# A fused two-block transformer layer: norm sums of queries and keys in two fp32r passes, and the softmax's last product on GpSimd

## The reference, cut to what matters

```python
q_ca = rmsnorm_2(hs(q_ca, N_CA_HEADS), g_q[l])     # x * rsqrt(mean(x*x over 64) + eps) * g
k_ca = rmsnorm_2(hs(k_ca, N_CA_HEADS), g_k[l])
s = einsum('bnqhd,bnkhd->bnhqk', qc, k_band) * d ** -0.5 + bias
p = softmax(where(valid, s, NEG_INF))
out = einsum('bnhqk,bnkhd->bnqhd', p, v_band)
```

## Time and profile before

| | |
|---|---|
| median of 3 runs | 955.28 us (955.16 to 955.39) |
| the profiled execution | 955.42 us |
| its span | 953.7 us |
| PE busy | 941.1 us (99%) |
| DVE, ACT, POOL busy | 691.2, 565.2, 103.8 us |
| TensorE clock granted | full in all 40 slices |
| chain that ended last | PE 86%, DVE 9%, ACT 3% |

### The profile page before, as it was taken

The page is one execution under the profiler, slowest core; times in us unless marked ns, Lnnn a source line. Parts: engine busy times, 40 slices in busy tenths (PEclk is TensorE's granted clock), DMA queues, the critical chain, the costliest instruction groups (busy, mean ns, idle before and its releaser), DMA issues.

```text
span 953.7 us, 13305 instructions
## 1 busy us (share of the span) xinstructions
PE 941.1 (99%) x4712; PEld 786.3 (82%) x4712; DVE 691.2 (72%) x1278; ACT 565.2 (59%) x1115; POOL 103.8 (11%) x215
## 2 busy tenths in 40 slices
PE   8999999999999999999999999999999999999998
PEld 7878998888888887877788877898888888888887
DVE  6487888878788766667768886856544853673988
ACT  6448787753223257479987664556745634644562
POOL 5001212211121103000000000110000000000110
PEclk9999999999999999999999999999999999999999
DMA  8233222149798743733442423365867567586773
GB/s 302 89 112 108 69 79 89 55 157 354 284 322 278 190 142 127 300 111 100 133 166 73 127 67 131 146 167 133 212 207 180 168 192 189 122 234 193 169 186 111
DMA packets 34963, 156.71 MB, mean 164 GB/s; under 512 B 5273, under 2 KB 5529, under 8 KB 22226
## 3 DMA queue, kind: packets, MB, share of 16 engines
q1 hardware_dynamic: 21106, 103.64, 31.6%
q0 software_dynamic: 11152, 49.29, 20.9%
q10 hardware_dynamic: 2640, 2.93, 0.9%
HBM read 144.61 MB, written 5.27 MB: 157 GB/s over the span
## 4 chain that ended last, share of the span: by engine, by line
PE 86%; DVE 9%; ACT 3%; issue 1%; DMA 1%; ACTq 0%; POOL 0%; DVEq 0%; POOLq 0%
PE psum L2276 26%; PE psum L2278 25%; PE psum L2277 25%; PE psum L2423 2%; PE psum L2450 2%; PE psum L2479 1%; PE psum L2474 1%; DVE wl L1318 1%; DVE p_sb L1518 1%; DMA raw<-in_wall 1%; DVE ptl L1537 1%; PE psum L2712 1%; DVE hl L1357 1%; DVE xt L1353 1%; DVE ah L1464 1%
## 5 line engine op out<-in xcount | busy, mean ns | idle before, releaser
L2276 PE MATMUL psum<-hh,wh 128*128 128x512 f32 (+2 forms) x736 | 277.7, 377 | 0.7 <-DVE hl L1357 0.6
L2278 PE MATMUL psum<-hh,wl 128*128 128x512 f32 (+2 forms) x736 | 270.2, 367 | 0.0
L2277 PE MATMUL psum<-hl,wh 128*128 128x512 f32 (+2 forms) x736 | 270.0, 367 | 0.0
L1318 DVE TENSOR_TENSOR wl<-raw,wh 128x512 fp32r<-128x512 f32 x336 | 218.7, 685 | 37.6 <-ACT wh L733 37.0
L733 ACT ACTIVATE wh<-raw 128x512 fp32r<-128x512 f32 x336 | 193.3, 621 | 68.3 <-PE psum L2278 65.2
L2276 PEld LDWEIGHTS psum<-hh,wh 128*128 128x128 f32 x736 | 138.5, 188 | 24.5 <-DVE hl L1357 1.8
L2278 PEld LDWEIGHTS psum<-hh,wl 128*128 128x128 f32 x736 | 138.4, 188 | 23.0
L2277 PEld LDWEIGHTS psum<-hl,wh 128*128 128x128 f32 x736 | 138.7, 188 | 20.5 <-issue 1.2
L2276 PE MATMUL psum<-wh,ah 128*128 128x512 f32 x192 | 76.1, 396 | 0.4 <-ACT p_sb L879 0.4
L2278 PE MATMUL psum<-wh,al 128*128 128x512 f32 x192 | 74.9, 390 | 0.0
L2277 PE MATMUL psum<-wl,ah 128*128 128x512 f32 x192 | 74.8, 389 | 0.0
(11 more groups left out here) (372 smaller groups left out, 1748.6 us busy)
## 6 DMA issues: line engine op xcount, KB each, us to landing
raw<-in_wall SPq DMA_DIRECT2D x79, 1024.0 KB, 5.4
raw<-in_wall POOLq DMA_DIRECT2D x20, 1024.0 KB, 8.1
wa<-in_wada POOLq DMA_DIRECT2D x24, 512.0 KB, 5.8
gt<-in_wada POOLq DMA_DIRECT2D x20, 512.0 KB, 6.9
xt<-in_xcols SPq DMA_DIRECT2D x8, 264.0 KB, 7.9
cb<-c_rows SPq DMA_DIRECT2D x8, 264.0 KB, 3.2
x<-in_x SPq DMA_DIRECT2D x4, 512.0 KB, 11.9
x_kept<-x SPq DMA_DIRECT2D x4, 512.0 KB, 2.6
```

The source lines that it names most:

```text
L1318: e.tensor_tensor(lower_, raw_of(w, c), upper_.bitcast(F32), ALU.subtract).then_inc(v["wl"], 1)
L2276: e.matmul(out_, lh, rh, start=start, stop=False, skip_group_check=True)
L2277: e.matmul(out_, lh, rl, start=False, stop=False, skip_group_check=True)
L2278: return e.matmul(out_, ll, rh, start=False, stop=stop, skip_group_check=True)
```

## The change: what it does

1. `blk` becomes fp32r. After the square ACT also copies it as fp32r into `sq_hi` (upper part), and 2 steps after the set's end (`LAG_LOW`) DVE subtracts that from the square into `sq_lo`. PE sums with two fp32r matmuls instead of one float32 matmul.
2. The lags grow: sum 2 to 4, root 3 to 5, norm 4 to 6 steps.
3. `normalize` of the CA heads moves from ACT (age 6) to POOL (age 5), as a `tensor_scalar` in float32 in place; the turn on PE waits for `g["norm"]`.
4. POOL's other work of the stage is now written into a loop over the steps: table blocks at steps 17, 33, 49, ..., the first value row at 31, `strip` at 72. A semaphore is shared to make room (`ss`), another renamed (`norm`).

```diff
-        LAG_SUM, LAG_ROOT, LAG_NORM = 2, 3, 4
+        LAG_LOW, LAG_SUM, LAG_ROOT, LAG_NORM = 2, 4, 5, 6
...
                     e.activation(sq[:, sub, :], bank[sub], ACT.Square).then_inc(a["sq"], 1)
+                    e.wait_ge(a["sq"], 4 * p + 2 * sub + 1)
+                    if p or sub:
+                        e.wait_ge(t["ss"], 2 * p + sub)
+                    e.activation(sq_hi, sq[:, sub, :], ACT.Copy).then_inc(a["sq"], 1)
...
+                if n - LAG_LOW in SQUARES:
+                    p, sub = SQUARES[n - LAG_LOW]
+                    e.wait_ge(a["sq"], 4 * p + 2 * sub + 2)
+                    if p or sub:
+                        e.wait_ge(t["ss"], 2 * p + sub)
+                    e.tensor_tensor(sq_lo, sq[:, sub, :], sq_hi.bitcast(F32), ALU.subtract).then_inc(v["ss"], 1)
                 if n - LAG_NORM in SQUARES:
...
+            def normalize(h, i):
+                mx, su, nmx = small(h, i)
+                e.wait_ge(v["rcp"], n_score(h, i))
+                e.tensor_scalar(block_p(h, i), block_p(h, i), mx, None, ALU.mult).then_inc(g["norm"], 1)
+
+            table_mask(8)
+            table_mask(9)
+            for n in range(steps_s):
+                if n == 31:
+                    first_value_row()
+                if n == 72:
+                    whole_sticks()
+                if n > 16 and n % 16 == 1:
+                    for x_ in beats_s[first_s[n - 17]:first_s[n - 1]]:
+                        if x_ and x_[0] == "S" and x_[2] == 0 and x_[1] + 2 in CA:
+                            table_mask(x_[1] + 2)
+                for b_ in range(first_s[n], first_s[n + 1]):
+                    x_ = beats_s[b_ - 5] if b_ > 4 else None
+                    if x_ and x_[0] == "S" and x_[1] in CA:
+                        normalize(*x_[1:])
...
                 if h in SB:
                     e.wait_ge(v["scan_s"], n_sb(h, i0))
+                elif h in CA:
+                    e.wait_ge(g["norm"], 12 + n_score(h, i0) - 32)
...
-                    e.wait_ge(a["sq"], 2 * p + sub + 1)
+                    e.wait_ge(v["ss"], 1 + 2 * p + sub + 1)
...
-                    e.matmul(bank[2], blk[:, :], sq[:, sub, :], start=True, stop=True).then_inc(t["ss"], 1)
+                    e.matmul(bank[2], blk[:, :], sq_hi, start=True, stop=False)
+                    e.matmul(bank[2], blk[:, :], sq_lo, start=False, stop=True).then_inc(t["ss"], 1)
```

More of the change, by code:

```diff
@@ L190, in program @@
         ones = sb("ones", [128, 128])
-        blk = sb("blk", [128, 128])
+        blk = sb("blk", [128, 128], F32R)
         eps = sb("eps", [128, 1])
@@ L205, in program @@
         br.close()
+        bq = ExitStack()
+        sb("under_q", [128, 3072], where=bq)
+        parts_q = sb("sq_parts", [128, 2, SEQ], F32R, where=bq)
+        bq.close()
         gt = sb("gt", [128, 2, D])
@@ L278, in program @@
         sq = two
+        sq_hi, sq_lo = parts_q[:, 0, :], parts_q[:, 1, :]
         v_rows = (rows[:, 3072:3584], rows[:, 3840:4352], v_end[:, 0:512], rows[:, 1024:1536])
@@ L920, in at @@
                     return flat[b_ - age] if b_ >= age else None
-                if (x_ := at(AGE["norm"])) and x_[0] == "S" and x_[1] not in SB:
+                if (x_ := at(AGE["norm"])) and x_[0] == "S" and x_[1] in FG:
                     normalize(*x_[1:])
@@ L1034, in keep @@
             def keep(i):
-                e.wait_ge(g["rs1"], 3 * i + 3)
+                e.wait_ge(g["norm"], 3 * i + 3)
                 e.activation(x1[:, i, :], scaled[:, i % 2, :], ACT.Copy, scale=sm[:, 128 + 2 * i:129 + 2 * i]).then_inc(a["xk"], 1)
@@ L2196, in _ @@
                 e.wait_ge(a["nsq"], 2 * i + 1)
-                e.tensor_scalar(r[:, 0:1], m1, EPS, None, ALU.add).then_inc(g["rs1"], 1)
+                e.tensor_scalar(r[:, 0:1], m1, EPS, None, ALU.add).then_inc(g["norm"], 1)
                 e.wait_ge(a["nsq"], 2 * i + 2)
[L2199 to L2202, removed]
+                e.wait_ge(g["norm"], 3 * i + 1)
+                e.tensor_scalar(r[:, 1:2], r[:, 0:1], EPS, m2, ALU.mult, ALU.add).then_inc(g["norm"], 1)
+                e.wait_ge(g["norm"], 3 * i + 2)
+                e.tensor_tensor(r, r, half[:, 0:2], ALU.pow).then_inc(g["norm"], 1)
             gate(0)
@@ L2206, in _, with table_mask @@
             e.wait_ge(v["m"], 24)
-            for h in CA:
+            def table_mask(h):
                 e.wait_ge(d[f"bt{h % 2}"], 16 * (h // 2 - 3))
                 e.memset(bt[h % 2][0:64, 448:512], NEG).then_inc(g["bt"], 1)
[L2210 to L2222, removed]
+            def first_value_row():
+                for j in range(4):
+                    e.wait_ge(d[f"x{4 + j}"], 32)
+                e.wait_ge(v["tile"], 48)
+                e.memset(dv[0][0:1, :], 0.0).then_inc(g["strip"], 1)
@@ new lines, in whole_sticks @@
+            def whole_sticks():
+                e.wait_ge(v["qn"], 8)
+                e.wait_ge(v["tile"], 40)
+                e.memset(strip[:, 0:384], 0.0).then_inc(g["strip"], 1)
+                e.memset(strip[:, 384:512], 1.0).then_inc(g["strip"], 1)
+                e.wait_ge(g["strip"], 3)
+                e.affine_select(out=strip[:, 384:512], in_=strip[:, 384:512], compare_op=ALU.is_ge, fill=0.0, base=0,
+                                pattern=[[1, 128]], channel_multiplier=-1).then_inc(g["strip"], 1)
```

14 lines of the change are left out of this document (7 added, 7 removed).

## The result

| | before | changed |
|---|---|---|
| median of 7 runs each, same chip | 955.39 us | 958.18 us |
| ratio | | 1.0028 (1.0019 to 1.0038) |
| profiled execution; its span | 955.42; 953.7 | 958.56; 956.8 |

A forecast was written before the change was run, and what follows sets the result against it. TensorE was taken as the bound. Terms −3.27 + 0.1 + 0.4 + 1.2 + 0.2 + 1.96 − 0.2 = +0.4 us on the profiled 955.42 gave 955.8, a median of 955.7 us; range 953.0 to 958.2.

The forecast's parts named there:

- (b): Rival: GpSimd's products and VectorE's splits and scores hinder each other, so norms come late; 958.5 us, chance 0.20.
- The sums: Eight norm sums on PE: two fp32r matmuls take 0.455 us instead of 0.863 for one float32; −3.27 us.
- Steps 16 and 24: PE waits there for the first and second norm, late on VectorE; +0.1 and +0.4 us.
- Head 8's first score: Step 33: PE arrives earlier but the copy of the keys' lower part hardly does; idle 0.82 to 2.0 us, +1.2.
- Head 8's first turn: Turns on PE wait for a POOL product, taken as 0.87 us for 512 columns; +0.2 us (0 to 1.0).
- Step 68: The last sum now stands directly before it, so PE waits 2.37 us instead of 0.41; +1.96 us.
- My own test: Forecast wrong as a whole if PE's waits between 395 and 475 us sum to under 2.5 or over 7 us.
- (a): Rival: waits at the norms and head 8's first score are absorbed, only step 68 costs, 1.2 us; 953.0 us, chance 0.23.
- (c): Rival: GpSimd's product takes 1.17 us or more, so turns wait at each of eight heads; 956.9 us, chance 0.10.
- Relief of ScalarE: ACT loses about 17.8 us of normalize and gets eight copies; a split wait may go; −0.2 us (−0.4 to +0.3).

The follow-up runs named there:

- keys_first: Changed kernel with ScalarE writing the keys' upper part ahead of the root and VectorE their lower part ahead of the norm; 955.13 us, ratio 1.0000.
- pool_only: Changed kernel with the norm sums as before (one float32 matmul, lags 2, 3, 4), products still on GpSimd; 955.50 us, ratio 1.0000.
- sums_only: Changed kernel with the softmax's last product back on ScalarE, two-pass sums and long lags kept; 959.38 us, ratio 1.0042.
- mid_f32_act: Changed kernel with lags 2, 3, 4, 5 for seven sums, the eighth float32 with lags 2, 3, 4, products on ScalarE; 958.19 us, ratio 1.0027.
- last_mid: Changed kernel with the eighth sum alone one step earlier (lags 2, 3, 4, 5); 957.93 us, ratio 1.0026.
- gap_before: Kernel before with longer lags (4, 5, 6) for the eighth norm sum only, still float32; 958.47 us, ratio 1.0028.
- last_short: Changed kernel with lags 1, 2, 3, 4 for the eighth sum only, still two fp32r passes; 956.04 us, ratio 1.0005.
- fill: Changed kernel plus five fp32r matmuls with unread results between the eighth sum and step 68; 956.85 us, ratio 1.0013.

## Why the prediction was right, and where it was wrong

The time lies in the range, 0.02 us from its upper end, and there by luck: that end was set near the value of rival (b), whose mechanism is not there. The forecast itself, 955.7, missed by 2.5 us; a kernel slower by over 0.2%, which came out, had a chance of 0.24.

- *The sums.* Right: L2752 and L2753 start 0.24 and 0.22 us ahead of what follows them, and a sum saves 0.41.

```profile
401.60 0.40 PE L2752 MATMUL psum<-sq_parts,blk 128*128 128x512 f32 x1
401.84 0.39 PE L2753 MATMUL psum<-sq_parts,blk 128*128 128x512 f32 x1
402.06 0.39 PE L2314 MATMUL psum<-hh,wh 128*128 128x512 f32 x1
```

- *Steps 16 and 24.* Right in mechanism: VectorE's norm passes end at 404.86 and 411.19, and the steps start behind them, at 404.92 and 411.25.

```profile
404.12 0.74 DVE L1814 SCALAR_TENSOR_TENSOR qk<-psum,prm,two 128x512 f32<-128x512 f32 x1
...
410.45 0.74 DVE L1814 SCALAR_TENSOR_TENSOR qk<-psum,prm,two 128x512 f32<-128x512 f32 x1
```

- *Head 8's first score.* Right: 1.7 for 2.0; keys_first shows the chain that it names.
- *Head 8's first turn.* The term that was mis-sized by five times. I took 0.87 us for a product of 512 columns between bounds of 0.53 and 1.17; the real ones of 512 columns took 1.73 us on average, above both, by form (count, sum, mean ns):

```profile
L2244 POOL TENSOR_SCALAR p_sb<-p_sb,sm 128x512 f32<-128x512 f32 x8 | 13.8, 1725 | 44.5 <-DVE sm L1518 44.5
L2244 POOL TENSOR_SCALAR p_sb<-p_sb,sm 128x384 f32<-128x384 f32 x8 | 11.4, 1422 | 2.6 <-DVE sm L1518 2.6
L2244 POOL TENSOR_SCALAR p_sb<-p_sb,sm 128x256 f32<-128x256 f32 x8 | 9.0, 1130 | 1.5 <-DVE sm L1518 1.4
L2244 POOL TENSOR_SCALAR p_sb<-p_sb,sm 128x128 f32<-128x128 f32 x8 | 5.9, 735 | 1.3 <-DVE sm L1518 1.2
```

The place was right, and it takes both, the length and the place. The reciprocal (425.58) stands behind the norm (424.92), the product starts at 425.85, and the turn waits until 427.49; in pool_only, where the reciprocal is ahead of the norm, the same product costs nothing:

```profile
424.92 0.75 DVE L1814 SCALAR_TENSOR_TENSOR qk<-psum,prm,two 128x512 f32<-128x512 f32 x1 [1.38 <-ACT two L1117]
425.58 0.15 DVE L1518 RECIPROCAL sm<-sm 128x1 f32<-128x1 f32 x1
...
427.49 0.33 PE L2490 MATMUL psum<-ident,p_sb 128*128 128x128 f32 x1 [0.77 <-POOL p_sb L2244]
```

The Trainium skill's 0.77 us for 512 columns, which it gives as a best case ("GPSIMD Engine Reference", §3.1), is half of what one of these took that stands alone (1.57 us at 445.91). Spans on GpSimd are rough in such traces, but the turn that waits (425.85 to 427.49, 1.64 us) bears this one out.

- *Step 68.* The wait is 2.41 for 2.37. **The step that failed is what follows from it**: I ended the account when PE starts again, at full speed. The clock that PE was granted behind the gap was half for 3.4 us, 1.56 us more. My own test, PE's waits summing to under 7 us, could not have found it, since they sum to about 5.3, and the 1.2 that it gives for the kernel before should be 1.6.
- *The rivals.* (a) fails: step 68 costs 2.0, not 1.2, and the wait before the first score grew from 0.8 to 1.7. (b) gives nearly the measured time by a mechanism that is not there: VectorE's splits between 421 and 510 us take 685 ns on average where they took 679, though GpSimd computes beside them; the subtraction has 737 on average for four, one of 0.87 and three of 0.69 among them. The subtraction at 446.88 starts a microsecond after a product has begun, right after ScalarE's copy that it needs, and takes its usual 0.69:

```profile
445.91 1.57 POOL L2244 TENSOR_SCALAR p_sb<-p_sb,sm 128x512 f32<-128x512 f32 x1 [4.47 <-DVE sm L1518]
...
446.88 0.69 DVE L1804 TENSOR_TENSOR sq_parts<-two,sq_parts 128x512 fp32r<-128x512 f32 x1 [0.27 <-ACT sq_parts L1149]
```

The Trainium skill ("SBUF — State Buffer", Terms) describes a lock held for a whole instruction, in which the loser fully blocks; VectorE as the loser for a product of 1.6 us is not what these rows show. (c) was right that the product is slow, and wrong on the place: only one turn waits, not one at each head.
- *Relief of ScalarE.* Hardly felt in the sum, but sums_only and mid_f32_act show that without it the change costs 1.2 us more (2.8 up to step 68, before the clock) and 2.2 us more: it pays for the copies that the two-pass sum brings.

## What to carry to other kernels

A matmul that is made cheaper by splitting its input lengthens the chain in front of it; price that chain from the last result to the consumer, queue by queue, before choosing a lag: here a lag too short cost 0.7 us a sum, one too long cost the wait behind it. A wait of PE as long as those here (2.1 us and more) should be priced with a clock term: here it was nothing in some executions and 1 to 3 us in others. Where the wait couldn't be removed, matmuls into a free bank within it kept the clock up. And an "issue" wait is worth following to the transfer that ends it: one exchange of order on VectorE and ScalarE won 1.9 us there, over half of what the eight sums save.

## What the runs showed of the hardware

- Kernels whose profile shows a wait of PE of 2.1 to 2.4 us had a lower mean clock (0.998 or less) in part of their executions: 7 of 7 (changed), 8 of 10 (last_mid), 5 of 11 (keys_first), 4 of 7 (gap_before). With 2.6 us in sums_only it was 1 of 5, with two more at 0.999. Where the longest wait is 1.7 us (last_short), and where five matmuls follow 1.0 us of waiting (fill), it was 0 of 11. Where between lies the change, and what decides in one execution, these runs don't tell; the length of the wait alone does not.
- In three profiles with a fall, half clock lasted 3.4 us (changed, 461.5 to 464.9), 3.4 us (last_mid, 460.4 to 463.8) and 6.8 us (keys_first, 458.0 to 464.8), with PE busy again for most or all of it. It began 2.9, 2.0 and 1.9 us after PE had come to a stop: once behind the wait and twice within it.
- GpSimd's float32 product with a scalar per partition takes 735 ns on average for 128 columns and about 330 more for each further 128 (L2244 above); ScalarE did the same in 390 to 715 ns (L873 in the kernel before, 128 and 512 columns).
